# Half FFNs with seven block products on one core: token sums before the gate tile, block sums merged, product P6 one place later

## Chip, core and metric

The kernel runs on one NeuronCore of a Trainium2 chip as a hand-ordered program: TensorE (PE), VectorE (DVE), ScalarE (ACT), GpSimd (POOL) and SyncE (SP) each have their own instruction list and meet only in semaphores. The metric is the device time of one execution in microseconds.

## The reference, cut

One inference step of two layers for 512 prompt tokens and 8 sample tokens, model width 1024. The change lies in the four half FFNs alone; the mixers between them (gated linear attention with DeltaNet, stick-breaking attention with RG-LRU) stay as they are.

```python
def half_ffn(x, g, w_gate, w_up, w_down):      # width 1024 -> 2816 -> 1024
    h = rmsnorm(x, g)
    return 0.5 * ((jax.nn.silu(h @ w_gate) * (h @ w_up)) @ w_down)

for layer in range(2):
    x = x + half_ffn(x, ...)                   # both for x_prompt and x_sample
    x = x + mixer(rmsnorm(x, ...))
    x = x + half_ffn(x, ...)
y = rmsnorm(x, ln_final)
```

## The kernel before

All 520 tokens are held transposed (features on partitions) in xT. A float32 operand is split into a high part, copied by ACT (hb_h, ht_h, whi, act_h), and the rest, subtracted by DVE (hb_l, ht_l, wlo, act_l). A product of two such operands is three matmuls: high x high, high x low, low x high. A tile of 128 output features over 1024 inputs and two halves of 260 tokens is 8 x 3 x 2 = 48 matmuls. The factor rstd of the norm is applied by DVE behind the matmuls.

The stages f0 to f3 run the same list, EVENTS. **The head**: gate tile and up tile of the features n = 0 to 3, each a plain tile ("unit") with an event of its own. DVE multiplies the gate tile by rstd (`take`), ACT applies silu, DVE multiplies by the up tile (`product`), ACT copies the high part (`high`), DVE subtracts (`low`). Each pass of n also prepares one quarter of the token sums: ACT scales a row block to xb, DVE makes four sums t1 to t4 in snapT, ACT copies them to ht_h, DVE subtracts to ht_l. t_act and t_dve count these steps; a pass starts its xb only when the ht_l of the pass in front is done, since snapT and xb have one buffer.

**The groups**: from feature tile 4 on, two gate tiles (2t, 2t+1) are made by seven block products P1 to P7 for the eight of a 2 x 2 block product (9 groups in a stage, 36 in all). A product is 12 matmuls into a PSUM bank of its own, bank_of; the group is 84 matmuls. DVE adds the products up in sums counted by block_sum: U2 = P1 + P6, U3 = U2 + P7, c11 = P1 + P2, c12 = U2 + P5 + P3, c22 = U3 + P5, c21 = U3 + P4. ACT has copied P1 to snapT before (p1_copied). Then follow the two up tiles of 48 matmuls, and the next group. After tiles 11 and 21 come the down products, 16 pieces each.

The weights of a group have four batches: a (for P1, P2), b (P4), c (P6, P5), d (P3, P7). Behind the splits of a and b DVE makes two block sums of weights each (line 1600), in place in the stage buffer; c and d need them. `make` on ACT and DVE makes the next batch in line, `ahead(done, last)` makes those whose slot is free by then, `reach(done)` waits until TensorE has finished an event. Every engine works strictly by its list, so the place of `ahead` among the other calls sets the order. TensorE starts the first group of a stage when t_dve says that the token sums of all four passes are done; it starts P3 after p1_copied, P7 after U2, P4 after c11, and the next group's P1 after all seven sums.

The lines of before that matter: ACT head 1012 to 1024 (silu 1002, high 1006, xb 1020, ht_h 1023) and copy of weights 959; DVE weight split 1608, weight sums 1600, take 1665, act_l 1674, product 1684, ht_l 1692, token sums 1708 to 1715, scaling by rstd 1729, block sums 1735; TensorE units 2505, block products 2526.

Of the kernel before, what the change touches and what calls it, by code (L numbers as in the profile page):

```python
# [33 lines left out]
P = 128  # L34
# [14 lines left out]
ORDER = ("P1", "P6", "P2", "P5", "P3", "P7", "P4")  # L49
# [57 lines left out]
def build_step(nc, i, o):  # L107
# [170 lines left out]
    with ctx:  # L278
# [305 lines left out]
        U2_SUM, C11_SUM, V_SUM, C12_SUM, U3_SUM, C22_SUM, C21_SUM = range(1, 8)  # L584
        BLOCK_SUMS = 7
# [360 lines left out]
        def _(act):  # L946
# [45 lines left out]
            def ffn(s, f):  # L992
# [19 lines left out]
                def head(n, up, done):  # L1012

                    ahead(done - 1)
                    if not up:
                        silu(n)
                        act.wait_ge(x_ready, KD * (s + 1))
                        if KP * f + n:
                            act.wait_ge(t_dve, 5 * (KP * f + n))
                        act.activation(xb[:], xT[:, 2 * n, :], ACT.Copy, scale=h_scale(s, 2 * n)).then_inc(t_act, 1)  # L1020
                    else:
                        act.wait_ge(t_dve, 5 * (KP * f + n) + 4)
                        act.activation(ht_h[:, :, n, :], snapT[:], ACT.Copy).then_inc(t_act, 1)
                        high(n)

                def group_step(g, which, t, up, done, late):
# [3 lines left out]
                    if which == "P1":  # L1030
                        reach(done)
                        if q:
                            act.wait_ge(block_sum, BLOCK_SUMS * (q - 1) + C11_SUM)
                        act.activation(snapT[:, 2, :], PS[:, bank_of("P1", up), 0:HALF], ACT.Copy).then_inc(p1_copied, 1)
                        ahead(done, own - 1)
                    elif which == "P2":
                        ahead(done, own)
                        if late:
                            half_of(*late.pop())
# [4 lines left out]
                    elif which == "P7":  # L1044
                        ahead(done, own + 3)
                        half_of(2 * t, up)
                    elif which == "P4":
# [545 lines left out]
        def _(dve):  # L1593
# [74 lines left out]
            def ffn(s, f):  # L1668
# [17 lines left out]

                def head(n, up, done):

                    ahead(done - 1)
                    if up:  # L1690
                        dve.wait_ge(t_act, X_TURNED + 2 * (KP * f + n) + 2)
                        dve.tensor_tensor(ht_l[:, :, n, :], snapT[:], ht_h[:, :, n, :].bitcast(F32), ALU.subtract)\  # L1692
                           .then_inc(t_dve, 1)
                    reach(done)
                    if not up:
# [6 lines left out]
                        count, x1, g1 = 5 * (KP * f + n), xT[:, 2 * n + 1, :], h_scale(s, 2 * n + 1)  # L1702
                        t1, t2, t3, t4 = (snapT[:, m, :] for m in range(4))
                        b11, b12, b21, b22 = xb[:, 0:HALF], xb[:, HALF:TOK], x1[:, 0:HALF], x1[:, HALF:TOK]
                        dve.wait_ge(t_act, X_TURNED + 2 * (KP * f + n) + 1)
                        if count:
                            dve.wait_ge(t_dve, count)
                        dve.tensor_tensor(t1, b12, b11, ALU.subtract).then_inc(t_dve, 1)
                        dve.scalar_tensor_tensor(out=t3, in0=b22, scalar=g1, in1=b12, op0=ALU.mult, op1=ALU.subtract)\
                           .then_inc(t_dve, 1)  # L1710
                        dve.wait_ge(t_dve, count + 1)
                        dve.scalar_tensor_tensor(out=t2, in0=b22, scalar=g1, in1=t1, op0=ALU.mult, op1=ALU.subtract)\
                           .then_inc(t_dve, 1)
                        dve.wait_ge(t_dve, count + 3)
                        dve.scalar_tensor_tensor(out=t4, in0=b21, scalar=g1, in1=t2, op0=ALU.mult, op1=ALU.subtract)\
# [7 lines left out]
                def half_of(n, up, q):  # L1723

                    dve.wait_ge(block_sum, BLOCK_SUMS * q + (C21_SUM if n % 2 else C12_SUM))
# [11 lines left out]
                def group_step(g, which, t, up, done, late):  # L1737
# [3 lines left out]
                    bank = {w: PS[:, bank_of(w, up), 0:HALF] for w in PRODUCTS}  # L1741
                    u2, u3, p1 = (snapT[:, n, :] for n in range(3))
                    (c11, c12), (c21, c22) = ([tmp[:, a + 2 * up, h * HALF:(h + 1) * HALF] for h in range(2)] for a in range(2))
# [745 lines left out]
        def _(pe):  # L2489
# [40 lines left out]
            def ffn(s, f):  # L2530
# [45 lines left out]
                def group_product(g, which, t, up):  # L2576
# [10 lines left out]
                    elif which == "P7":  # L2587
                        pe.wait_ge(block_sum, BLOCK_SUMS * q + U2_SUM)
                    elif which == "P4":
                        pe.wait_ge(block_sum, BLOCK_SUMS * q + C11_SUM)  # L2590
# [737 lines left out]
```

## Time and profile before

| | us |
|---|---|
| median of 3 runs | 2202.9 |
| lowest and highest | 2197.45, 2203.23 |
| profiled execution, whole | 2199.94 |
| its span, first to last instruction | 2198.3 |
| TensorE busy | 2129.5 (97%) |
| DVE busy | 1352.5 (62%) |
| ACT busy | 861.6 (39%) |
| mean granted TensorE clock | 0.985 of full |

The profiled execution is one run of its own. Its span leaves out 1.6 us of start and end. Where TensorE is busy nearly all the time, the profile is to be read for the places where it isn't: the list of its waits, the chain of work that ended last, and then the timelines of DVE and ACT around such a place.

### The profile page before, as it was taken

To read this page: it belongs to the slowest core of one execution; us is meant where nothing else is said; L and a number is where in the kernel's file an instruction comes from. 1 tells how busy PE (TensorE), PEld (TensorE's weight loads), DVE (VectorE), ACT (ScalarE), POOL (GpSimd) and SP (SyncE) were. 2 spreads that over 40 slices of the span, in tenths; PEclk is the share of its full clock that TensorE was granted. 3 is DMA by queue.
4 is the path that set the end of the run, shared out by engine and by line. 5 is a ranking of instruction groups with operands and counts; after the bars stand their busy time and mean duration, and the time that the engine had idled before them with its cause. 6 is when DMAs were issued, how large, how long until landed. Compare 5 with 4: busy or idle time off the path is not lost.

```text
span 2198.3 us, 42097 instructions
## 1 busy us (share of the span) xinstructions
PE 2129.5 (97%) x17908; PEld 2070.3 (94%) x17908; DVE 1352.5 (62%) x2124; ACT 861.6 (39%) x1232; POOL 67.2 (3%) x140
## 2 busy tenths in 40 slices
PE   7899999999988999999999999999999999999998
PEld 7899999999978899999999999999997599999997
DVE  6763675686455557737656754675657547745754
ACT  5431332344244444313334332333457634322323
POOL 0000000100100000000000000000102300000000
PEclk9999999999998999999999999999999999999999
DMA  4332232533200333332323232332324423232321
GB/s 148 89 103 83 84 106 70 132 83 85 75 10 2 82 91 97 106 92 87 95 79 115 78 106 87 106 92 82 102 78 131 140 78 106 78 110 82 113 74 64
DMA packets 318362, 199.16 MB, mean 91 GB/s; under 512 B 10006, under 2 KB 313266, under 8 KB 318168
## 3 DMA queue, kind: packets, MB, share of 16 engines
q1 hardware_dynamic: 309840, 174.49, 27.0%
q0 software_dynamic: 6160, 19.84, 3.1%
q8 instruction: 142, 2.33, 0.4%
q10 hardware_dynamic: 2176, 2.15, 0.3%
q14 instruction: 44, 0.36, 0.1%
HBM read 188.52 MB, written 8.05 MB: 89 GB/s over the span
## 4 chain that ended last, share of the span: by engine, by line
PE 87%; DVE 7%; ACT 3%; issue 3%; DMA 0%; ACTq 0%; DVEq 0%
PE PS L2505 60%; PE PS L2526 17%; PE PS L2678 4%; DVE wlo L1608 1%; PE PS L3220 1%; ACT whi L959 1%; PE PS L3139 1%; PE PS L3153 0%; DVE ht_l L1692 0%; PE PS L3122 0%; ACT xb L1020 0%; DVE tmp L1665 0%; DVE X L2052 0%; PE PS L3205 0%; PE PS L3023 0%
## 5 line engine op out<-in xcount | busy, mean ns | idle before, releaser
L2505 PE MATMUL PS<-hb_h,whi 128*128 128x260 f32 x2448 | 498.2, 285 | 1.8 <-DVE hb_l L2430 1.8
L2505 PE MATMUL PS<-hb_h,wlo 128*128 128x260 f32 x2448 | 496.1, 284 | 0.0
L2505 PE MATMUL PS<-hb_l,whi 128*128 128x260 f32 x2448 | 493.9, 283 | 0.0
L2505 PEld LDWEIGHTS PS<-hb_h,whi 128*128 128x128 f32 x2448 | 380.7, 189 | 4.5 <-DVE wlo L1608 1.4
L2505 PEld LDWEIGHTS PS<-hb_h,wlo 128*128 128x128 f32 x2448 | 378.7, 189 | 0.0
L2505 PEld LDWEIGHTS PS<-hb_l,whi 128*128 128x128 f32 x2448 | 377.5, 189 | 0.0
L1608 DVE TENSOR_TENSOR wlo<-stage,whi 128x1024 fp32r<-128x1024 f32 (+1 forms) x193 | 232.6, 1205 | 151.1 <-ACT whi L959 145.5
L959 ACT ACTIVATE whi<-stage 128x1024 fp32r<-128x1024 f32 (+1 forms) x193 | 199.9, 1038 | 123.3 <-PE PS L2526 64.4
L1608 DVE TENSOR_TENSOR wlo<-stage_x,whi 128x1024 fp32r<-128x1024 f32 (+1 forms) x148 | 175.1, 1185 | 52.2 <-ACT whi L959 51.9
L959 ACT ACTIVATE whi<-stage_x 128x1024 fp32r<-128x1024 f32 (+1 forms) x148 | 150.8, 1022 | 133.4 <-DVE stage_x L1600 115.2
L1813 DVE SCALAR_TENSOR_TENSOR tmp<-PS,rstd 128x520 f32<-128x520 f32 x64 | 44.7, 698 | 235.8 <-PE PS L2505 235.8
L2505 PE MATMUL PS<-act_l,whi 128*128 128x260 f32 x896 | 180.8, 283 | 0.0
L2505 PE MATMUL PS<-act_h,wlo 128*128 128x260 f32 x896 | 180.1, 282 | 0.0
L2505 PE MATMUL PS<-act_h,whi 128*128 128x260 f32 x896 | 179.9, 282 | 0.0
L2526 PE MATMUL PS<-hb_h,whi 128*128 128x260 f32 x432 | 124.0, 287 | 17.5 <-DVE ht_l L1692 17.5
L2505 PEld LDWEIGHTS PS<-act_h,wlo 128*128 128x128 f32 x896 | 138.1, 188 | 0.0
L2505 PEld LDWEIGHTS PS<-act_h,whi 128*128 128x128 f32 x896 | 138.0, 188 | 0.0
L2505 PEld LDWEIGHTS PS<-act_l,whi 128*128 128x128 f32 x896 | 137.7, 188 | 0.0
L2526 PE MATMUL PS<-hb_l,whi 128*128 128x260 f32 x432 | 123.5, 286 | 0.0
L2526 PE MATMUL PS<-ht_h,whi 128*128 128x260 f32 x432 | 123.5, 286 | 0.0
L2526 PE MATMUL PS<-ht_l,whi 128*128 128x260 f32 x432 | 123.5, 286 | 0.0
L2526 PE MATMUL PS<-hb_h,wlo 128*128 128x260 f32 x432 | 123.5, 286 | 0.0
(472 smaller groups left out, 3764.2 us busy)
## 6 DMA issues: line engine op xcount, KB each, us to landing
stage<-in_ffn_w_up SPq DMA_DIRECT2D x88, 512.0 KB, 3.8
stage_x<-in_ffn_w_gate SPq DMA_DIRECT2D x36, 1024.0 KB, 5.2
stage<-in_w_in_e SPq DMA_DIRECT2D x28, 512.0 KB, 3.8
stage_x<-in_ffn_w_down SPq DMA_DIRECT2D x20, 512.0 KB, 4.2
stage<-in_ffn_w_down SPq DMA_DIRECT2D x40, 256.0 KB, 2.7
stage<-in_w_in_o SPq DMA_DIRECT2D x20, 512.0 KB, 3.8
stage<-in_ffn_w_gate SPq DMA_DIRECT2D x16, 512.0 KB, 3.8
stage_x<-in_ffn_w_down SPq DMA_DIRECT2D x20, 384.0 KB, 3.7
```

The source lines that it names most:

```text
L959: act.activation(split_out(batch, False), staged(batch), ACT.Copy).then_inc(hi_ready, 1)
L1608: dve.tensor_tensor(split_out(batch, True), staged(batch), split_out(batch, False).bitcast(F32), ALU.subtract).then_inc(lo_ready, 1)
L1813: dve.scalar_tensor_tensor(out=y, in0=psum, scalar=0.5, in1=two(rstd[:]), op0=ALU.mult, op1=ALU.mult)\
L2505: mm = pe.matmul(psum[:, half, :], w, x(k, half), start=first and w is hi and x is rhs_hi, stop=last and w is lo)
L2526: mm = pe.matmul(PS[:, bank, 0:HALF], w[:, c:c + P], x[:, j, :], start=j == 0 and n == 0, stop=j == KP - 1 and n == 2)
L2678: return pe.matmul(out, w, x, start=True, stop=True)
L3139: mm = pe.matmul(acc, upto[:], sp[:, at:at + w], start=True, stop=n == NB - 1)
L3220: return pe.transpose(dst, src, ident[0:n, 0:n])
```

## The change

Three things are changed; all that is computed stays, up to the order of additions.

1. In the head, DVE makes the token sums of pass n at the start of the event of gate tile n (new `token_sums`), before the weight batches and before `take`, and ht_l directly behind `take`. ACT makes xb first, then the weight copy that is due, then ht_h, and silu behind it.
2. The seven block sums are five. P1_SUMS adds P1 to P2 and P6 in one operation over two banks (c11 and U2 at once, U2 in the place of c12). U3, V and C12 follow behind P4, and C2_SUMS adds U3 to P4 and P5 in one (c21, c22). P7 and P4 both wait for P1_SUMS.
3. ORDER is P1, P2, P6, P5, ...: P2 and P6 change places, and their banks too. The late silu or high of the tile in front stays at the third product; silu of tile 2t comes with P4 and no longer with P7.

```diff
-ORDER = ("P1", "P6", "P2", "P5", "P3", "P7", "P4")
+ORDER = ("P1", "P2", "P6", "P5", "P3", "P7", "P4")
-            return 4 * up + {"P1": 0, "P6": 1, "P2": 2, "P5": 3, "P3": 0, "P7": 1, "P4": 2}[which]
+            return 4 * up + {"P1": 0, "P2": 1, "P6": 2, "P5": 3, "P3": 0, "P7": 1, "P4": 2}[which]
...
                 def head(n, up, done):
-                    ahead(done - 1)
                     if not up:
-                        silu(n)
                         act.wait_ge(x_ready, KD * (s + 1))
                         if KP * f + n:
                             act.wait_ge(t_dve, 5 * (KP * f + n))
                         act.activation(xb[:], xT[:, 2 * n, :], ACT.Copy, scale=h_scale(s, 2 * n)).then_inc(t_act, 1)
-                    else:
+                    ahead(done - 1)
+                    if not up:
                         act.wait_ge(t_dve, 5 * (KP * f + n) + 4)
                         act.activation(ht_h[:, :, n, :], snapT[:], ACT.Copy).then_inc(t_act, 1)
+                        silu(n)
+                    else:
                         high(n)
...
                 def head(n, up, done):
+                    if not up:
+                        token_sums(n)
                     ahead(done - 1)
-                    if up:
-                        dve.wait_ge(t_act, X_TURNED + 2 * (KP * f + n) + 2)
-                        dve.tensor_tensor(ht_l[:, :, n, :], snapT[:], ht_h[:, :, n, :].bitcast(F32), ALU.subtract)\
-                           .then_inc(t_dve, 1)
                     reach(done)
...
                         take(two(tmp[:, n % 2, :]), pair(2 * (n % 2))).then_inc(gate_read, 1)
...
+                        dve.wait_ge(t_act, X_TURNED + 2 * (KP * f + n) + 2)
+                        dve.tensor_tensor(ht_l[:, :, n, :], snapT[:], ht_h[:, :, n, :].bitcast(F32), ALU.subtract)\
                            .then_inc(t_dve, 1)
...
-                    elif which == "P2":
+                    elif which == "P6":
                         reach(done)
-                        if q:
-                            dve.wait_ge(block_sum, BLOCK_SUMS * q)
                         dve.wait_ge(p1_copied, q + 1)
-                        add(q, U2_SUM, u2, p1, bank["P6"])
                         if base + 2 * t >= 2:
                             dve.wait_ge(act_lo if up else prod_ready, base + 2 * t - 1)
-                        add(q, C11_SUM, c11, p1, bank["P2"])
+                        add(q, P1_SUMS, tile0, PS[:, first + 1:first + 3, 0:HALF], p1.to_broadcast([P, 2, HALF]))
                         ahead(done, own)
...
                     elif which == "P3":
-                        reach(done)
-                        add(q, V_SUM, c12, u2, bank["P5"], U2_SUM)
-                        add(q, C12_SUM, c12, c12, bank["P3"], V_SUM)
-                        half_of(2 * t, up, q)
                         ahead(done, own + 2)
                     elif which == "P7":
-                        reach(done)
-                        add(q, U3_SUM, u3, u2, bank["P7"])
-                        dve.wait_ge(act_lo if up else prod_ready, base + 2 * t)
-                        add(q, C22_SUM, c22, u3, bank["P5"], U3_SUM)
                         ahead(done, own + 3)
                     elif which == "P4":
                         reach(done)
-                        add(q, C21_SUM, c21, u3, bank["P4"])
+                        add(q, U3_SUM, snapT[:, 1, :], PS[:, bank_of("P7", up), 0:HALF], c12, P1_SUMS)
+                        add(q, V_SUM, c12, PS[:, bank_of("P5", up), 0:HALF], c12, U3_SUM)
+                        add(q, C12_SUM, c12, PS[:, bank_of("P3", up), 0:HALF], c12, V_SUM)
+                        dve.wait_ge(act_lo if up else prod_ready, base + 2 * t)
+                        add(q, C2_SUMS, tile1, PS[:, first + 2:first + 4, 0:HALF], u3.to_broadcast([P, 2, HALF]))
+                        half_of(2 * t, up, q)
                         half_of(2 * t + 1, up, q)
...
-                    elif which == "P7":
-                        pe.wait_ge(block_sum, BLOCK_SUMS * q + U2_SUM)
-                    elif which == "P4":
-                        pe.wait_ge(block_sum, BLOCK_SUMS * q + C11_SUM)
+                    elif which in ("P7", "P4"):
+                        pe.wait_ge(block_sum, BLOCK_SUMS * q + P1_SUMS)
```

The order on DVE in the head of f0, pass n = 1, before (take, four token sums, weight split, ht_l, product, act_l):

```order
L1665 SCALAR_TENSOR_TENSOR tmp<-PS,rstd 128x520 [waits unit_done]
L1708 TENSOR_TENSOR snapT<-xb 128x260 [waits t_dve,t_act]
L1709 SCALAR_TENSOR_TENSOR snapT<-xT,prm,xb 128x260
L1712 SCALAR_TENSOR_TENSOR snapT<-xT,prm,snapT 128x260 [waits t_dve]
L1715 SCALAR_TENSOR_TENSOR snapT<-xT,prm,snapT 128x260 [waits t_dve]
L1608 TENSOR_TENSOR wlo<-stage,whi 128x1024 [waits unit_done,hi_ready]
L1692 TENSOR_TENSOR ht_l<-snapT,ht_h 128x4x260 [waits t_act]
L1684 TENSOR_TENSOR tmp<-tmp,PS 128x520 [waits gate_ready,unit_done]
```

and after the change, from the token sums of the same pass to its product:

```order
L1696 TENSOR_TENSOR snapT<-xb 128x260 [waits t_dve,t_act]
L1697 SCALAR_TENSOR_TENSOR snapT<-xT,prm,xb 128x260
L1700 SCALAR_TENSOR_TENSOR snapT<-xT,prm,snapT 128x260 [waits t_dve]
L1703 SCALAR_TENSOR_TENSOR snapT<-xT,prm,snapT 128x260 [waits t_dve]
L1609 TENSOR_TENSOR wlo<-stage,whi 128x1024 [waits unit_done,hi_ready]
L1666 SCALAR_TENSOR_TENSOR tmp<-PS,rstd 128x520 [waits unit_done]
L1720 TENSOR_TENSOR ht_l<-snapT,ht_h 128x4x260 [waits t_act]
L1609 TENSOR_TENSOR wlo<-stage,whi 128x1024 [waits unit_done,hi_ready]
L1685 TENSOR_TENSOR tmp<-tmp,PS 128x520 [waits gate_ready,unit_done]
```

The four sums stand in front of the weight split and take, and ht_l stands behind take; the second weight split of the pass is now behind ht_l.

The order on ACT in the same pass, before (silu, xb, weight copy, ht_h, act_h, weight copy):

```order
L1002 ACTIVATE tmp<-tmp 128x520 [waits gate_read]
L1020 ACTIVATE xb<-xT,prm 128x520 [waits t_dve,x_ready]
L959 ACTIVATE whi<-stage 128x1024 [waits unit_done,w_loaded0]
L1023 ACTIVATE ht_h<-snapT 128x4x260 [waits t_dve]
L1006 ACTIVATE act_h<-tmp 128x520 [waits prod_ready]
L959 ACTIVATE whi<-stage 128x1024 [waits unit_done,w_loaded1]
```

and after:

```order
L1018 ACTIVATE xb<-xT,prm 128x520 [waits t_dve,x_ready]
L959 ACTIVATE whi<-stage 128x1024 [waits unit_done,w_loaded1]
L1022 ACTIVATE ht_h<-snapT 128x4x260 [waits t_dve]
L1002 ACTIVATE tmp<-tmp 128x520 [waits gate_read]
L959 ACTIVATE whi<-stage 128x1024 [waits unit_done,w_loaded0]
L1006 ACTIVATE act_h<-tmp 128x520 [waits prod_ready]
```

xb stands in front, silu behind ht_h. Both silu and ht_h wait for DVE.

The order on DVE in the first group, before, from U2 and c11 (rows 1 and 2) on:

```order
L1735 TENSOR_TENSOR snapT<-snapT,PS 128x260 [waits p1_copied,unit_done]
L1735 TENSOR_TENSOR tmp<-snapT,PS 128x260 [waits prod_ready]
L1608 TENSOR_TENSOR wlo<-stage,whi 128x1024 [waits unit_done,hi_ready]
L1608 TENSOR_TENSOR wlo<-stage_x,whi 128x1024 [waits unit_done,hi_ready]
L1600 TENSOR_TENSOR stage_x<-stage_x 128x4x128 [waits lo_ready]
L1600 TENSOR_TENSOR stage_x<-stage_x 128x4x128 [waits sums]
L1608 TENSOR_TENSOR w4l<-stage_x,w4h 128x512 [waits unit_done,hi_ready]
L1600 TENSOR_TENSOR stage_x<-stage_x 128x4x128 [waits sums,lo_ready]
L1600 TENSOR_TENSOR stage_x<-stage_x 128x4x128 [waits sums]
L1735 TENSOR_TENSOR tmp<-snapT,PS 128x260 [waits block_sum,unit_done]
L1735 TENSOR_TENSOR tmp<-tmp,PS 128x260 [waits block_sum]
L1729 TENSOR_TENSOR tmp<-tmp,rstd 128x520 [waits block_sum]
```

and after, from P1_SUMS (row 1) on:

```order
L1740 TENSOR_TENSOR tmp<-PS,snapT 128x520 [waits prod_ready,p1_copied,unit_done]
L1609 TENSOR_TENSOR wlo<-stage,whi 128x1024 [waits unit_done,hi_ready]
L1609 TENSOR_TENSOR wlo<-stage_x,whi 128x1024 [waits unit_done,hi_ready]
L1601 TENSOR_TENSOR stage_x<-stage_x 128x4x128 [waits lo_ready]
L1601 TENSOR_TENSOR stage_x<-stage_x 128x4x128 [waits sums]
L1609 TENSOR_TENSOR w4l<-stage_x,w4h 128x512 [waits unit_done,hi_ready]
L1601 TENSOR_TENSOR stage_x<-stage_x 128x4x128 [waits sums,lo_ready]
L1601 TENSOR_TENSOR stage_x<-stage_x 128x4x128 [waits sums]
L1609 TENSOR_TENSOR wlo<-stage_x,whi 128x1024 [waits unit_done,hi_ready]
L1740 TENSOR_TENSOR snapT<-PS,tmp 128x260 [waits block_sum,unit_done]
L1740 TENSOR_TENSOR tmp<-PS,tmp 128x260 [waits block_sum] x2
L1740 TENSOR_TENSOR tmp<-PS,snapT 128x520 [waits prod_ready]
```

One sum of 520 elements stands where U2 and c11 stood, the weight batches follow it directly, and all other block sums come behind them.

## Rows read from the trace of the kernel before

**Rows 1.** The page: busy time by engine; the chain that ended last, by engine.
```profile
PE 2129.5 (97%) x17908; PEld 2070.3 (94%) x17908; DVE 1352.5 (62%) x2124; ACT 861.6 (39%) x1232; POOL 67.2 (3%) x140
...
PE 87%; DVE 7%; ACT 3%; issue 3%; DMA 0%; ACTq 0%; DVEq 0%
```

**Rows 2.** Waits of TensorE (total us, times, longest): all, 60 to 80, 780 to 1300.
```profile
PE PS L2526 <- DVE ht_l L1692: 17.5, 4, 7.0
...
PE PS L2526 <- DVE ht_l L1692: 7.0, 1, 7.0
...
PE PS L2526 <- DVE ht_l L1692: 6.2, 2, 4.3
```

**Rows 3.** The chain in order of time: start us, us, what; behind the four heads.
```profile
75.92 11.64 PE PS L2526 x84
...
99.08 10.08 PE PS L2526 x84
...
849.39 11.87 PE PS L2526 x84
...
1221.07 11.84 PE PS L2526 x84
...
1856.84 11.87 PE PS L2526 x84
```

**Rows 4.** Windows: length, busy us of PE, PEld, DVE, ACT, POOL, PEclk, DMA share, GB/s.
```profile
1223.00:1225.00 2.00, 2.00 (x11) 2.00 (x10) 0.59 (x2) 1.33 (x2) 0.00 (x0) 0.50 0.69 246
...
880.00:1100.00 220.00, 220.00 (x1836) 220.00 (x1836) 136.17 (x194) 70.45 (x93) 0.00 (x0) 1.00 0.32 94
```

**Rows 5.** DVE in order of time in the head of f0: start us, us, what [idle before].
```profile
43.56 0.69 DVE L1684 TENSOR_TENSOR tmp<-tmp,PS 128x520 f32<-128x520 f32 x1
...
53.12 0.69 DVE L1684 TENSOR_TENSOR tmp<-tmp,PS 128x520 f32<-128x520 f32 x1
...
55.27 0.49 DVE L1638 MEMSET ssum<- 128x520 f32 x1
...
58.77 0.43 DVE L1708 TENSOR_TENSOR snapT<-xb 128x260 f32<-128x260 f32 x1 [1.32 <-ACT xb L1020]
...
60.44 1.22 DVE L1608 TENSOR_TENSOR wlo<-stage_x,whi 128x1024 fp32r<-128x1024 f32 x1
...
65.08 1.23 DVE L1692 TENSOR_TENSOR ht_l<-snapT,ht_h 128x1040 fp32r<-128x1040 f32 x1
...
74.62 1.24 DVE L1692 TENSOR_TENSOR ht_l<-snapT,ht_h 128x1040 fp32r<-128x1040 f32 x1
```

**Rows 6.** ACT in order of time in the heads of f0, f1 and f2.
```profile
36.92 1.28 ACT L990 ACT_TABLE_LOAD   x1
...
44.28 0.64 ACT L1006 ACTIVATE act_h<-tmp 128x520 fp32r<-128x520 f32 x1 [1.91 <-DVE tmp L1684]
44.83 1.04 ACT L959 ACTIVATE whi<-stage 128x1024 fp32r<-128x1024 f32 x1
...
58.02 0.71 ACT L1020 ACTIVATE xb<-xT,prm 128x520 f32<-128x520 f32 x1
...
60.56 1.08 ACT L1023 ACTIVATE ht_h<-snapT 128x1040 fp32r<-128x1040 f32 x1 [0.35 <-DVE snapT L1715]
...
807.41 1.28 ACT L990 ACT_TABLE_LOAD   x1
...
1181.42 1.28 ACT L990 ACT_TABLE_LOAD   x1
```

**Rows 7.** One group from 99.08 on, DVE and ACT; idle of DVE before line 1735 until.
```profile
103.44 0.43 DVE L1735 TENSOR_TENSOR snapT<-snapT,PS 128x260 f32<-128x260 f32 x1 [0.28 <-PE PS L2526]
...
109.65 1.42 DVE L1600 TENSOR_TENSOR stage_x<-stage_x 128x512 f32<-128x512 f32 x2
...
112.64 0.64 ACT L1002 ACTIVATE tmp<-tmp 128x520 f32<-128x520 f32 x1 [1.15 <-DVE tmp L1729]
...
  PE PS L2526: 18.8, 36
```

More of the change, by code:

```diff
@@ L583, in build_step @@
         block_sum, p1_copied = sem("block_sum"), sem("p1_copied")
-        U2_SUM, C11_SUM, V_SUM, C12_SUM, U3_SUM, C22_SUM, C21_SUM = range(1, 8)
-        BLOCK_SUMS = 7
+        P1_SUMS, U3_SUM, V_SUM, C12_SUM, C2_SUMS = range(1, 6)
+        BLOCK_SUMS = 5
         t_act, t_dve = sem("t_act"), sem("t_dve")
@@ L1037, in group_step @@
                         ahead(done, own)
-                        if late:
-                            half_of(*late.pop())
+                    elif which == "P6" and late:
+                        half_of(*late.pop())
                     elif which == "P5":
@@ L1045, in group_step @@
                         ahead(done, own + 3)
+                    elif which == "P4":
                         half_of(2 * t, up)
-                    elif which == "P4":
                         late.append((2 * t + 1, up))
@@ L1685, in product, with token_sums @@
                        .then_inc(prod_ready, 1)
+                def token_sums(n):
+                    count, x1, g1 = 5 * (KP * f + n), xT[:, 2 * n + 1, :], h_scale(s, 2 * n + 1)
+                    t1, t2, t3, t4 = (snapT[:, m, :] for m in range(4))
+                    b11, b12, b21, b22 = xb[:, 0:HALF], xb[:, HALF:TOK], x1[:, 0:HALF], x1[:, HALF:TOK]
+                    dve.wait_ge(t_act, X_TURNED + 2 * (KP * f + n) + 1)
+                    if count:
+                        dve.wait_ge(t_dve, count)
+                    dve.tensor_tensor(t1, b12, b11, ALU.subtract).then_inc(t_dve, 1)
+                    dve.scalar_tensor_tensor(out=t3, in0=b22, scalar=g1, in1=b12, op0=ALU.mult, op1=ALU.subtract)\
+                       .then_inc(t_dve, 1)
+                    dve.wait_ge(t_dve, count + 1)
+                    dve.scalar_tensor_tensor(out=t2, in0=b22, scalar=g1, in1=t1, op0=ALU.mult, op1=ALU.subtract)\
+                       .then_inc(t_dve, 1)
+                    dve.wait_ge(t_dve, count + 3)
+                    dve.scalar_tensor_tensor(out=t4, in0=b21, scalar=g1, in1=t2, op0=ALU.mult, op1=ALU.subtract)\
+                       .then_inc(t_dve, 1)
                 def head(n, up, done):
+                    if not up:
+                        token_sums(n)
                     ahead(done - 1)
-                    if up:
-                        dve.wait_ge(t_act, X_TURNED + 2 * (KP * f + n) + 2)
-                        dve.tensor_tensor(ht_l[:, :, n, :], snapT[:], ht_h[:, :, n, :].bitcast(F32), ALU.subtract)\
-                           .then_inc(t_dve, 1)
                     reach(done)
@@ L1740, in group_step @@
                     own = BY_FIRST[f, g, "a"].n + (6 if MODES[t][1] == "P" else 4)
-                    bank = {w: PS[:, bank_of(w, up), 0:HALF] for w in PRODUCTS}
-                    u2, u3, p1 = (snapT[:, n, :] for n in range(3))
-                    (c11, c12), (c21, c22) = ([tmp[:, a + 2 * up, h * HALF:(h + 1) * HALF] for h in range(2)] for a in range(2))
+                    first = 4 * up
+                    u3, p1 = snapT[:, 1:2, :], snapT[:, 2:3, :]
+                    tile0, tile1 = two(tmp[:, 2 * up, :]), two(tmp[:, 2 * up + 1, :])
+                    c12 = tmp[:, 2 * up, HALF:TOK]
                     if which == "P1":
                         ahead(done, own - 1)
-                    elif which == "P2":
+                    elif which == "P6":
                         reach(done)
-                        if q:
-                            dve.wait_ge(block_sum, BLOCK_SUMS * q)
                         dve.wait_ge(p1_copied, q + 1)
-                        add(q, U2_SUM, u2, p1, bank["P6"])
                         if base + 2 * t >= 2:
                             dve.wait_ge(act_lo if up else prod_ready, base + 2 * t - 1)
-                        add(q, C11_SUM, c11, p1, bank["P2"])
+                        add(q, P1_SUMS, tile0, PS[:, first + 1:first + 3, 0:HALF], p1.to_broadcast([P, 2, HALF]))
                         ahead(done, own)
```

19 lines of the change are left out of this document (2 added, 17 removed).

## The prediction

> **What bounds the kernel now.** The first view is busy time by engine with the chain that ended last [rows 1]. TensorE is busy for 2129.5 of 2198.3 us and carries 87% of the chain, DVE 7%. Only idle time of TensorE, or its time at a lower clock, is to be had. The list of TensorE's waits comes second [rows 2]: its largest entry is 17.5 us before the first block product (line 2526) of the four feed-forward stages, released by DVE's ht_l at line 1692. It splits into 7.0 us (stage f0), 6.2 us together in f1 and f2, and 4.3 us in f3; the last two stages of the sum are 4.3 for f1 (the longest of that answer) and 1.9 for f2. In the chain by pieces [rows 3] the 84 matmuls of a group take 10.08 us each time, but 11.64, 11.87, 11.84 and 11.87 us right behind the four stalls. The windows behind the stall of f2 show why: the granted clock is 0.50 from 1223 to 1225, that is 1.2 instead of 2.4 GHz, after 1.9 us idle, and 1.00 over 220 us of unbroken groups [rows 4]. This adds 1.56 + 1.79 + 1.76 + 1.79 = 6.9 us. The stalls thus cost 17.5 + 6.9 = 24.4 us. That is everything which the first part of the change can win.
>
> **Where the stall comes from.** TensorE may start the first group only when the token sums of all four passes are split (t_dve), so the end of the last ht_l counts. In f0 that is 75.86 [rows 5], with TensorE free since 75.92 - 7.0 = 68.9. From the product of pass 0 (starts 43.56) to the end of the last ht_l DVE takes 32.3 us for three passes. In each pass DVE idles 1.32 us for xb [rows 5], since ACT runs silu first and can do that only after DVE's take; it idles again for act_h and for a weight copy.
>
> **Part 1, token sums ahead of the gate tile.** The work stays the same; its order changes. I put the new order together from the old durations. Steps on DVE follow each other some 0.1 us before the end of the row in front, ACT's too; I use start to start. From the start of product(n): 0.69 for it, 0.64 - 0.10 for high(n), 0.71 for xb(n+1) and about 0.1 of hand-over give 2.0 us to the first token sum, and act_l now lies in that time, not ahead of it. The four sums take 60.44 - 58.77 = 1.67 us, a weight split 1.22 less the overlap, 1.15, take 0.7 (as long as the product, 520 elements from PSUM), silu 0.54 (as act_h, 0.64 less the overlap), then ACT's weight copy 1.04 [rows 5, 6] and DVE's split of it 1.15: 2.0 + 1.67 + 1.15 + 0.7 + 0.54 + 1.04 + 1.15 = 8.25 us to product(n+1), where it is 53.12 - 43.56 = 9.56 us now [rows 5]. ht_h on ACT (1.08) lies beside split and take, ht_l (1.24) beside silu and copy. From product(1) to product(2) the memset adds 0.45 (0.49 less a little) and the longer weight piece (a and b with their four block sums, 65.08 - 60.44 = 4.64 us, for 1.15) adds 3.5: 12.2 us. From product(2) to the end of ht_l(3): 2.0 + 1.67 + 1.15 + 0.6 + 1.24 = 6.7 us, because the split for d no longer stands in front. Together 8.25 + 12.2 + 6.7 = 27.15 us for 32.3.
>
> The start is the cost. xb(0) begins when the table load ends, 36.92 + 1.28 = 38.2 in f0 [rows 6], and now sums and take follow, then silu, weight copy and split: 0.75 + 1.67 + 0.7 + 0.4 (silu stands behind ht_h) + 0.6 + 1.04 + 1.15 = 6.3 us, so product(0) starts at 44.5, 0.9 us later than the 43.56 of before. The last ht_l ends at 44.5 + 27.15 = 71.65: **f0 keeps a stall of 71.65 - 68.9 = 2.75 us and saves 4.3**. In between, the third gate tile needs its weights at 68.9 - 4 x 5.76 = 45.8 (a tile has 48 matmuls of 10.08 / 84 = 0.12 us [rows 3]); the split now lands at 44.6. 1.2 us are left: cover, but thin.
>
> f1: table load over at 807.41 + 1.28 = 808.7 [rows 6], a weight piece more ahead of take, so 7.0 us to product(0) and 27.15 to the last ht_l: 842.85. TensorE is free at 849.39 - 4.3 = 845.1: 2.2 us of slack, **4.3 us saved and the clock kept, 1.79**. f3 stands to its own stall as f1 does (4.3, 11.87) and gives the same. f2: 1182.7 + 6.3 + 27.15 = 1216.15 against 1221.07 - 1.9 = 1219.2: 3 us of slack, **1.9 + 1.76 saved**. For f0 the clock is between kept and lost; the nearest row is f2, where 1.9 us idle cost 1.76, so I let f0 pay its 1.56.
>
> Sum: 4.3 + (4.3 + 1.79) + (1.9 + 1.76) + (4.3 + 1.79) = 20.1 us.
>
> The Trainium skill (TensorE: Matmul & The Clock Gate, Part 1: The HAM clock gate) advises that the ramp penalty is under 1% of a span and not to be fitted. Here it is 0.3% of the span, so the page agrees in size, yet it is over a quarter of the gain: left out, the sum would be 14.8 us.
>
> **Part 2, five sums for seven, and P6 a product later.** The path through TensorE is never held up by the block sums before: DVE idled for the end of the third product in all 36 groups, 18.8 us together, and the only wait of TensorE in line 2526 is the one for ht_l [rows 2, 7]. The merged first sum starts where U2 did, 103.44 in the group that starts at 99.08, and writes 520 elements from PSUM, as line 1684 does in 0.69 us. It ends at 104.15. P7, which waits for it, is the sixth product: 99.08 + 5 x 1.44 = 106.28. Slack 2.1 us for 2.4 before. DVE's pieces a and b still come behind it (the third order excerpt), so nothing new is in front. The other sums move behind P4: 3 x 0.42 + 0.69 and two scalings by rstd of 0.69 are 3.3 us, from about 112.8 (109.65 + 1.42 for the weight sums, the copy for c and its split) to 115.9. The banks are wanted by the next P1 at 99.08 + 10.08 + 11.52 = 120.7, two up tiles later: 4.8 us left. silu(2t) moves from 112.64 to about 115.4 and product(2t) stands behind it at about 116.1, where TensorE has finished its up tile at 109.16 + 5.76 = 114.9 [rows 3, 7]; the unit whose bank it frees is a whole group away. The last piece ahead of the next group, d, moves about 0.5 us and has over 5 us. Summed: nothing on the path; DVE loses 36 x (7 x 0.42 - 3 x 0.42 - 2 x 0.69) = 11 us of busy time, worth nothing. If the 2.1 us cover were gone, each microsecond late would cost 36. P6's weights get 1.44 us more time; they were never late, so nothing again. The queue of weight loads on SP keeps its order; slot 0 or its like comes free one product (1.44 us) sooner, which ACT uses for a copy 1.44 us earlier.
>
> The Trainium skill (Perfetto Trace Analysis, Optimizing Scalar/DVE Operations) speaks against this part: where DVE isn't saturated but makes another engine wait, splitting instructions lets work finish sooner. Merging does the reverse. By that rule the sum would be that of rival D; [rows 7] show that the condition, an engine that waits, does not hold here yet.
>
> **Rivals.**
> (B) No stall anywhere, f0 included: my 8.25 us per pass is 0.9 us too long. Against it: f0's start penalty and a chain made of measured rows. It gives 20.1 + 2.75 + 1.56 = 24.4 us, 2177.
> (C) Shorter stalls stay in f1 and f3 as well, since a hand-over or a weight copy is later than I have it by more than 2.2 us; then their clock loss stays too. Gain 4.3 + 3.7 + 2 x 2 = 12 us, 2190. For it: the slack is a sum of twenty terms. The thin 1.2 us at the third gate tile of f0 belongs here.
> (D) P7 ends up waiting for the first sum in every group, and each wait is longer by what the merged sum takes more, 0.69 - 0.42 = 0.27 us: 36 x 0.27 = 10 us given back, 2192. Against it: the 2.1 us of slack.
> (E) Slower: P7 waits for the first sum behind weight work. That needs a piece of kind a or b in front of it, 1.23 + 1.42 + 0.69 + 1.42 = 4.76 us less 2.1 of slack, 2.6 us x 36 = 95 us, 2277. It decides from 2.1 us on, and the gain is used up at 2.1 + 20/36 = 2.7 us. Against it: in the excerpt that work stands behind the sum.
> (F) The change doesn't reach the path: ACT's silu or high is really what ends the head, and product(0)'s 0.9 us recurs in each pass. Then f0 gains 1.5 us and the others 3.5 together: 2197. Against it: ACT idles between its steps of the head, since it waits for DVE's sums (0.35) [rows 6].
>
> **How the numbers follow.** The profiled run took 2199.9 us, span 2198.3; 2199.9 - 20.1 = 2179.8. The median is 3 us higher, 2202.9, which gives 2182.8. Neither is better, so 2181.5, and the rivals are counted from the same base, 2201.6. Chances: forecast 0.60, B 0.12, C 0.13, D 0.04, E 0.04, F 0.07. The range runs from B with the lowest run of before (2197.5 - 24.4 = 2173) to D and C, 2192. What a measurement of this kernel can tell from no change is about 0.3%, 6.6 us, so faster means below 2196.3: faster 0.88, same 0.07, slower 0.05.
>
> **What would show it.** In the profile after: TensorE's wait for ht_l is one entry of about 2.75 us in f0; groups behind the heads of f1, f2 and f3 take 10.08 us; DVE's idle before the first token sum is gone; three passes from product(0) to the last ht_l last some 27 us; no wait on a block sum. The forecast is wrong if line 2526 waits in 36 places, if any head unit waits for wlo, or if a group takes over 10.08 us while the head is clean.

## The result, and the profile after

| | before | after |
|---|---|---|
| median, us | 2201.65 (2197.45 to 2203.23, 4 runs) | 2178.59 (2177.07 to 2182.29, 4 runs) |
| profiled execution, whole | 2199.94 | 2179.37 |
| its span | 2198.3 | 2177.7 |
| mean granted clock | 0.985 | 0.990 |

The ratio is 0.9902, 95% interval 0.9885 to 0.9919: faster by 1%. The forecast was 2181.5, its range 2173 to 2192.

The page after, busy time by engine and the chain by engine, to be set beside [rows 1]; below it the only wait of line 2526, over the whole run, beside [rows 2]:

```profile
PE 2121.8 (97%) x17908; PEld 2062.7 (95%) x17908; DVE 1344.2 (62%) x2052; ACT 865.3 (40%) x1232; POOL 67.2 (3%) x140
...
PE 91%; DVE 5%; ACT 2%; issue 1%; DMA 0%; ACTq 0%; DVEq 0%
```

```profile
PE PS L2526 <- DVE ht_l L1720: 2.9, 1, 2.9
```

TensorE has less to wait for, so its share of the chain rises from 87 to 91%, and its busy time falls by 7.7 us although it issues the same 17908 matmuls: fewer of them run at the low clock. Four stalls of 17.5 us together have become one of 2.9 us. The chain in order of time (start, us, what) has the groups behind the four heads, beside [rows 3]; the second one is the ordinary group behind f0's:

```profile
71.66 11.86 PE PS L2526 x84
...
95.04 10.07 PE PS L2526 x84
...
837.30 10.07 PE PS L2526 x84
...
1205.25 10.08 PE PS L2526 x84
...
1838.05 10.08 PE PS L2526 x84
```

Only f0 still pays for the low clock. DVE in order of time in the head of f0 (start, us, line, operation, [idle before]), beside [rows 5]; line 1696 is the first token sum, 1685 the product, 1720 ht_l:

```profile
44.33 0.69 DVE L1685 TENSOR_TENSOR tmp<-tmp,PS 128x520 f32<-128x520 f32 x1
...
46.35 0.43 DVE L1696 TENSOR_TENSOR snapT<-xb 128x260 f32<-128x260 f32 x1
...
49.77 1.23 DVE L1720 TENSOR_TENSOR ht_l<-snapT,ht_h 128x1040 fp32r<-128x1040 f32 x1
51.51 1.23 DVE L1609 TENSOR_TENSOR wlo<-stage,whi 128x1024 fp32r<-128x1024 f32 x1 [0.51 <-ACT whi L959]
52.65 0.69 DVE L1685 TENSOR_TENSOR tmp<-tmp,PS 128x520 f32<-128x520 f32 x1
...
64.94 0.69 DVE L1685 TENSOR_TENSOR tmp<-tmp,PS 128x520 f32<-128x520 f32 x1
...
70.37 1.23 DVE L1720 TENSOR_TENSOR ht_l<-snapT,ht_h 128x1040 fp32r<-128x1040 f32 x1
```

The idle time of 1.32 us ahead of the token sums [rows 5] is gone. What is left in a pass is 0.70 us of waiting for ACT's high part of the product and 0.51 us for ACT's weight copy behind ht_l.

In one ordinary group, the merged first sum of DVE (line 1740), and behind P4 the last one, the answer on line 1740 as to what DVE waited for, beside [rows 7]:

```profile
99.39 0.70 DVE L1740 TENSOR_TENSOR tmp<-PS,snapT 128x520 f32<-128x520 f32 x1 [0.28 <-PE PS L2526]
...
109.59 0.69 DVE L1740 TENSOR_TENSOR tmp<-PS,snapT 128x520 f32<-128x520 f32 x1
...
  PE PS L2526: 16.3, 36
```

DVE still waits for the third product in all 36 groups, and TensorE never waits for the sum: its only wait in line 2526 is the one for ht_l.

### The profile page after: what moved, and what is told of

Its sections match the earlier page's. It is cut to its first block, busy times and chain, and to the rows that moved or that the text cites. A ratio compares the mean times of both kernels' runs of the same rounds, so it can differ in the third digit from the quotient of the medians.

```text
span 2177.7 us, 41989 instructions
## 1 busy us (share of the span) xinstructions
PE 2121.8 (97%) x17908; PEld 2062.7 (95%) x17908; DVE 1344.2 (62%) x2052; ACT 865.3 (40%) x1232; POOL 67.2 (3%) x140
## 4 chain that ended last, share of the span: by engine, by line
PE 91%; DVE 5%; ACT 2%; issue 1%; DMA 0%; ACTq 0%; DVEq 0%
PE PS L2505 65%; PE PS L2526 17%; PE PS L2676 4%; PE PS L3218 1%; PE PS L3137 1%; DVE wlo L1609 1%; PE PS L3151 0%; PE PS L3120 0%; DVE X L2052 0%; PE PS L3203 0%; PE PS L3140 0%; PE PS L3021 0%; ACT whi L959 0%; PE PS L2516 0%; PE PS L2744 0%
## 5 line engine op out<-in xcount | busy, mean ns | idle before, releaser
L2526 PE MATMUL PS<-ht_h,wlo 128*128 128x260 f32 x432 | 122.0, 283 | 0.0
```

Of the source, the lines that this page charges most:

```text
L2526: mm = pe.matmul(PS[:, bank, 0:HALF], w[:, c:c + P], x[:, j, :], start=j == 0 and n == 0, stop=j == KP - 1 and n == 2)
```

## Where the 20.6 us of span went

The numbers are read from the two chains in order of time. In f0 the stall ends 4.26 us sooner (71.66 against 75.92) and the first group is 0.22 us longer; f1 and f3 save 4.3 + 1.8 us each, f2 1.9 + 1.76. That is 19.9 of 20.6 us. The remaining 0.7 us is what is left of larger changes outside the heads, in code that is the same in both kernels. In the first layer the products ahead of the mixer came out 1.5 us shorter (185.44 for 186.98) and the mixer 2.2 us shorter (154.65 for 156.88). In the second layer the mixer came out 1.5 us longer (110.23 for 108.69) and so did the 432 matmuls behind it (53.43 for 51.90). In the windows over these stretches the granted clock falls at other places than before. This is looked at again below.

## The experiments

Each kernel is before or the change with the edit shown. They ran in three sets, each on one chip, with the kernel before beside them: e1 to e4 (before 2199.93, 15 runs), e5 and e6 (2197.37, 1 run), e7 to e10 (2198.68, 11 runs).

**1. Which part gives the gain.** `e1_head_only` takes from the change only the two `head` functions and `token_sums`; the block sums and ORDER are those of before. `e2_groups_only` is the rest.

> The new head alone (xb first on ACT, token sums ahead of take, ht_l behind it); order of products and the seven block sums as before. Theory: the whole gain is in the head, so 20 to 23 us below the kernel before, as the full change: one wait for ht_l of about 2.9 us in f0, none in f1, f2 and f3, and the first groups of f1 to f3 at 10.08 us. Rival (the merged sums help TensorE as well): clearly less gain than the full change, 3 us or more apart.

> The new groups alone (P6 a product later, five block sums); the head as before. Theory: nothing, within 0.2% of the kernel before; four waits for ht_l of 7.0, 4.3, 1.9 and 4.3 us and four first groups of 11.6 to 11.9 us stay, DVE is busy some 8 to 11 us less. Rival (merging gives something back or costs): 5 us or more either way, and a wait on a block sum or weights in line 2526.

| | median, us | ratio, 95% interval |
|---|---|---|
| e1_head_only | 2175.27 | 0.9891 (0.9876 to 0.9907) |
| e2_groups_only | 2200.82 | 1.0004 (0.9994 to 1.0013) |

Both expectations came true within the intervals (24.7 us for the 20 to 23 of the first), and the whole gain is the head's. TensorE's waits on ht_l, first of e1, then of e2:

```profile
PE PS L2531 <- DVE ht_l L1720: 3.0, 1, 3.0
```

```profile
PE PS L2521 <- DVE ht_l L1692: 17.5, 4, 7.1
```

**2. The place of ht_l on DVE.** In the full change ht_l goes back behind the weight work, directly ahead of the product; all else of the new order stays:

```diff
                         take(two(tmp[:, n % 2, :]), pair(2 * (n % 2))).then_inc(gate_read, 1)
-                        dve.wait_ge(t_act, X_TURNED + 2 * (KP * f + n) + 2)
-                        dve.tensor_tensor(ht_l[:, :, n, :], snapT[:], ht_h[:, :, n, :].bitcast(F32), ALU.subtract)
...
                     ahead(done - 1)
+                    if up:
+                        dve.wait_ge(t_act, X_TURNED + 2 * (KP * f + n) + 2)
+                        dve.tensor_tensor(ht_l[:, :, n, :], snapT[:], ht_h[:, :, n, :].bitcast(F32), ALU.subtract)
                     reach(done)
```

> The full change, but ht_l stands where it did, behind the second weight batch of its pass and ahead of the product. This parts the two edits in the head. Theory: the passes keep their 8.3 us, and only the last ht_l ends one split later, about 1.15 to 1.7 us (it waits for ACT's copy too): f0 waits 4.1 to 4.6 us instead of 2.9, f1 to f3 still not at all (slack was 2.3 us or more by the profile after). Rival (the place of ht_l is most of the gain): waits come back in f1 and f3, 2 us or more each with their clock loss, 8 us or more in all.

Measured 2201.86 us (one run): the expectation of +1.2 to 1.7 us failed, the rival holds, and the whole gain is gone. TensorE's waits, and one pass of DVE in f0:

```profile
PE PS L2527 <- DVE ht_l L1713: 21.4, 4, 9.3
```

```profile
48.47 0.69 DVE L1666 SCALAR_TENSOR_TENSOR tmp<-PS,rstd 128x520 f32<-128x520 f32 x1
50.82 1.23 DVE L1609 TENSOR_TENSOR wlo<-stage,whi 128x1024 fp32r<-128x1024 f32 x1 [1.65 <-ACT whi L959]
51.96 1.24 DVE L1713 TENSOR_TENSOR ht_l<-snapT,ht_h 128x1040 fp32r<-128x1040 f32 x1
53.11 0.69 DVE L1685 TENSOR_TENSOR tmp<-tmp,PS 128x520 f32<-128x520 f32 x1
```

Behind take DVE can do nothing on the product's way until ACT has done silu and the weight copy. In the change ht_l stands there, and 0.51 us of idle time are left. Here the whole 1.65 us are idle and ht_l's 1.15 us come on top. The product is thus 1.15 us later in each of the first three passes (the pass shown takes 9.46 us instead of 8.32; before it took 9.56), and the last ht_l, which TensorE waits for, also has the copy and the split in front: 8.29 us behind its product instead of 5.43. The sum, 1.15 + 1.14 + 1.17 + 2.86 = 6.3 us, matches the difference of the stalls in f0, 9.3 against 2.9. In f1 and f3 the slack of 2.1 us (experiment 4) swallows a part and 4.3 us of wait remain, to the tenth those of before; in f2 it is 3.5 us, where before had 1.9.

**3. ACT's order without DVE's.** The kernel before with the new order on ACT alone (xb, weight copy, ht_h, silu):

> Only ACT's new order in the head (xb, weight copy, ht_h, silu); DVE keeps take, token sums, weight split, ht_l of before, and the groups are those of before. It tells ACT's part of the head from DVE's. By the durations seen: product 0.69, act_l and hand-over 0.7, xb and weight copy on ACT in that time and 0.9 behind it, split 1.15, take 0.7, sums 1.67, split 1.15, ht_l 1.15: 8.7 us per pass for 9.56, and product(0) of f0 0.6 us earlier. The last ht_l comes 3.2 us sooner: waits of 3.8 us in f0, 1.1 in f1 and f3, none in f2; 11.5 us and one to three clock losses saved, 2183 to 2188. Rival: DVE's order is all of it (ht_l in the gap behind take, as its being moved away cost all that was won); then passes stay at 9.5 us and the time at 2197 to 2201.

Measured 2230.72 us, ratio 1.0141 (1.0113 to 1.0170): neither. It is 32 us **slower** than before. TensorE's waits, and a pass of DVE in f0:

```profile
PE PS L2527 <- DVE ht_l L1693: 46.2, 4, 14.5
```

```profile
52.02 0.49 DVE L1716 SCALAR_TENSOR_TENSOR snapT<-xT,prm,snapT 128x260 f32<-128x260 f32 x1
55.12 1.23 DVE L1609 TENSOR_TENSOR wlo<-stage,whi 128x1024 fp32r<-128x1024 f32 x1 [2.61 <-ACT whi L959]
56.27 1.23 DVE L1693 TENSOR_TENSOR ht_l<-snapT,ht_h 128x1040 fp32r<-128x1040 f32 x1
57.42 0.69 DVE L1685 TENSOR_TENSOR tmp<-tmp,PS 128x520 f32<-128x520 f32 x1
```

My sum of 8.7 us per pass had counted the DVE work and forgotten what stands on ACT in front of the copy that this split needs: ht_h (1.07) and silu (0.62), which begin only when DVE's last token sum is done, then the copy (1.04). DVE idles 2.61 us for it, with ht_l behind the idle time instead of in it. The pass takes 57.42 - 46.05 = 11.37 us (product to product) for 9.56. 28.7 us of the 32 are in the list of waits (46.2 against 17.5), 1.0 in the four first groups (48.2 against 47.2 us), the rest lies outside the heads.

e8 and e4 have the same order on ACT, and ht_l directly ahead of the product in both. In the heads they differ only in DVE's token sums (the groups' part is worth nothing by e2), behind take in e8 and ahead of the weight work in e4. With the sums ahead the time goes from 32 us above its kernel before to 2 us above, and f0's pass from 11.37 to 9.46 us. On the new order of ACT the early sums are thus worth some 30 us, and the place of ht_l some 22 us more; the order of ACT without the two costs 32 us. The gain belongs to the three together and can't be given to one of them. Two orders were not tried: DVE's new order with ACT's old one, and ht_l behind the product, which would tell whether it needs the wait or only has to be out of the product's way.

**4. How much room the heads have.** In the full change three more ht_l of the last pass stand ahead of the true one, each waiting for the one in front:

```diff
+                        for k in range(3 if n == 3 else 0):
+                            padded(dve.tensor_tensor(ht_l[:, :, n, :], snapT[:], ht_h[:, :, n, :].bitcast(F32), ALU.subtract))
                         dve.tensor_tensor(ht_l[:, :, n, :], snapT[:], ht_h[:, :, n, :].bitcast(F32), ALU.subtract)
```

> The full change, and DVE makes the subtraction of ht_l in pass 3 four times instead of once, in each of the four stages: 3 x 1.28 = 3.8 us later. Theory: the slack of the heads is 2.3 us (f1, f3) and 3 us (f2), so waits of about 6.7 us in f0, 1.5 us in f1 and f3 and 0.9 us in f2, and each of them costs the clock behind it too (first groups of 11.6 to 11.9 us instead of 10.08). Sum: 3.8 + 1.5 + 0.9 + 1.5 + 3 x 1.8 = 13 us above the full change. Rival (a stall under 2 us leaves the clock up): the same waits, first groups of f1 to f3 at 10.08 us, 8 us above.

Measured 2190.99 us (one run), 12 us over the change, for the 13 expected. The waits came out near the expectation (1.8 for 1.5 us, 1.0 for 0.9), the clock did not: the expectation had it fall behind all of them, the rival behind none in f1 to f3. The waits are 6.8 us in f0 (+3.9, the full delay), and in f1, f2 and f3:

```profile
PE PS L2536 <- DVE ht_l L1730: 1.8, 1, 1.8
...
PE PS L2536 <- DVE ht_l L1730: 1.0, 1, 1.0
```

(f3 has 1.8 again.) With 3.9 us of delay the slack is 3.9 - 1.8 = 2.1 us in f1 and f3 and 2.9 in f2; the prediction had 2.2 and 3. The first groups are 12.24, 11.84, 10.34 and 10.34 us. Waits (11.4 against 2.9) and groups (44.76 against 42.09) make 8.5 + 2.7 = 11.2 of the 11.6 us. The windows show f1, then f3 (length, busy us of PE, PEld, DVE, ACT, POOL, PEclk, DMA share, GB/s):

```profile
842.00:844.00 2.00, 0.66 (x6) 0.46 (x4) 1.97 (x2) 0.00 (x0) 0.00 (x0) 1.00 0.00 0
844.00:846.00 2.00, 1.53 (x8) 1.54 (x9) 2.00 (x3) 0.00 (x0) 0.00 (x0) 0.67 0.05 12
846.00:848.00 2.00, 2.00 (x11) 2.00 (x11) 0.85 (x2) 1.33 (x3) 0.00 (x0) 0.50 0.52 127
1846.00:1848.00 2.00, 0.70 (x6) 0.49 (x5) 1.97 (x2) 0.00 (x0) 0.00 (x0) 1.00 0.00 0
1848.00:1850.00 2.00, 1.50 (x12) 1.50 (x13) 2.00 (x3) 0.00 (x0) 0.00 (x0) 1.00 0.00 0
1850.00:1852.00 2.00, 2.00 (x19) 2.00 (x18) 0.88 (x2) 1.78 (x4) 0.00 (x0) 1.00 0.46 103
```

Both stages idle 1.8 us. Behind it the clock is at its lower level (1.2 GHz) in f1 and stays at 2.4 GHz in f3. Idle time of this size may or may not cost the clock; in f2, where 1.0 us were idle, it stayed up too.

**5. How much room the first block sum has, and what a repeated wait costs.** In front of P1_SUMS stand 4, 6 or 8 dependent additions of 260 elements each in a part of snapT that is free then, in all 36 groups:

```diff
+                        for k in range(4):
+                            padded(dve.tensor_tensor(snapT[:, 0, :], snapT[:, 2, :], snapT[:, 2, :], ALU.add))
                         add(q, P1_SUMS, tile0, PS[:, first + 1:first + 3, 0:HALF], p1.to_broadcast([P, 2, HALF]))
```

> The full change, and in each of the 36 groups four extra DVE sums of 260 elements stand in front of the first block sum: 4 x 0.45 = 1.8 us later. Theory: P7 has 2.1 us of slack for that sum, so no wait in line 2526 but the one of f0, and the time of the full change within 3 us. Rival (the sum is on the path already): 36 x 1.8 = 65 us more.

> As the run with four, with six extra sums in front of the first block sum: 2.7 us later, 0.6 us past the slack. Theory: 36 waits of about 0.6 us before P7, 20 us above the full change with the clock up. Rival (each such wait pulls the clock down as in the heads): 36 x (0.6 + 1.8) = 86 us above.

> As above with eight extra sums: 3.6 us later, 1.5 us past the slack. Theory: 36 waits of about 1.5 us, 54 us above the full change with the clock up. Rival (the clock falls with each, as behind the 1.9 us wait of f2 in the kernel before): 36 x (1.5 + 1.8) = 119 us above.

| additions | us (one run each) | over the change's profiled run |
|---|---|---|
| 4 | 2179.43 | 0.1 |
| 6 | 2213.30 | 33.9 |
| 8 | 2247.20 | 67.8 |

TensorE's waits for the sum, with 6 and then with 8 additions; 4 have none:

```profile
PE PS L2536 <- DVE tmp L1748: 24.7, 36, 0.7
```

```profile
PE PS L2536 <- DVE tmp L1748: 58.1, 36, 1.6
```

Two additions make 0.93 us per group (58.1 - 24.7 over 36), one 0.46. Six are 2.78 us and the wait is 0.69 (24.7 / 36), so the slack of P7 is 2.1 us, as forecast. The idle time also came out near 20 and 54 us. But these were the forecasts of the whole loss, and that was 33.9 and 67.8 us, 14 us more than forecast each time. The runs are 33.9 - 24.7 = 9.2 and 67.8 - 58.1 = 9.7 us longer than their idle time: each wait costs about **0.26 us more than its idle time**, in both runs. The chain shows where, with 6 additions and with 8 alike: the 24 matmuls behind the wait take 3.15 us, where 24 of an ordinary group take 2.88 (10.08 x 24/84).

```profile
103.82 3.15 PE PS L2536 x24
```

It is also what a first group with the clock kept has over 10.08 us (10.34 in experiment 4, 10.33 below). And 36 waits of 1.6 us, one in each group, cost no clock; the window over seven of the groups with 8 additions:

```profile
880.00:1100.00 220.00, 208.72 (x1727) 207.24 (x1726) 148.64 (x221) 66.45 (x86) 0.00 (x0) 1.00 0.31 94
```

**6. The last stall.** f0's first xb needs no rstd, only x. In the change, and later in the head part alone, it is made ahead of the norm, and `head` leaves it out where s and n are both 0:

```diff
             make()
+            act.wait_ge(x_ready, KD)
+            act.activation(xb[:], xT[:, 0, :], ACT.Copy, scale=h_scale(0, 0)).then_inc(t_act, 1)
             for s, (name, f) in enumerate(STAGES):
                 norm(s)
```

> The full change, and in f0 ACT makes xb of pass 0 before the norm instead of behind its last table load. Theory: the 2.9 us stall that f0 keeps comes from the late start of pass 0. The sums of pass 0 are then done before rstd, ht_h starts at the end of the table load (38.1), silu 1.0 later, weight copy and split behind it: product(0) at 41.7 instead of 44.3, the last ht_l 2.6 us sooner, stall 0.3 us or none; 2.6 us less than the full change, and 4.4 us less if the clock stays up as well. Rival (the head is bound elsewhere, by weights or by take waiting for TensorE): the last ht_l moves by under 1 us and the time stays that of the full change.

> The head part alone, and the xb of f0's first pass made before the norm instead of behind the table load; the groups are those of before. Theory: parts add up. The head alone keeps one stall in f0 (3.0 us in its trace) and a first group of 11.86 instead of 10.08 us; with the early xb the same head had a wait of 0.4 us and a first group of 10.33 us in the trace of the other run. So 2.6 + 1.5 = 4.1 us below the head alone of this call. Rival: what f0 gains is given back in the stretches up to the first mixer, and the two stay within 1.5 us, as the medians of the call before had it (2176.33 with both changes and early xb, 2175.27 for the head alone).

> The full change again, on the same chip as the head alone. Theory: the groups' part is worth nothing also on top of the head, and the difference between 2178.6 (full change) and 2175.3 (head alone) lies between chips and in the mixers: the two within 1 us of each other here. Rival: with the stalls gone the merged sums cost something, and the full change is 2 to 4 us above the head alone again.

> The head part alone again, the groups of before. Theory: the same as the full change within 1 us, 0.990 of before. Rival: 2 to 4 us below the full change.

| | median, us | lowest, highest | ratio, 95% interval |
|---|---|---|---|
| e3: change + early xb (first set) | 2176.33 | 2174.57, 2177.62 | 0.9898 (0.9883 to 0.9913) |
| e9: change | 2179.30 | 2179.09, 2179.86 | 0.9908 (0.9889 to 0.9926) |
| e10: head alone | 2177.63 | 2175.22, 2181.03 | 0.9900 (0.9880 to 0.9921) |
| e7: head alone + early xb | 2172.75 | 2171.63, 2172.93 | 0.9876 (0.9854 to 0.9898) |

e7 is the best kernel of the study, 26 us below the kernel before and 6.5 below the change on the same chip. Its wait, and f0's first group:

```profile
PE PS L2534 <- DVE ht_l L1723: 0.4, 1, 0.4
```

```profile
69.08 10.33 PE PS L2534 x84
```

The stall goes from 2.9 to 0.4 us and the group from 11.86 to 10.33, clock kept: 2.5 + 1.53 = 4.0 us. By the medians of e7 and e10 it is 4.9; the runs of the two don't overlap, the intervals of their ratios do. e3 shows the same two rows (0.4 and 10.33), and its median is 2.3 us below the change's of another set, for 2.6 to 4.4 expected. Yet it is 1.1 us above that of e1, the head alone in the same set. The traces place this at the very start, ahead of f0's stall: e1's matmuls behind the loading of x start at 22.5 us and e3's at 24.7, since the first pairs of matmuls, from 13 to 18 us, take 0.64 us each in e3 and 0.40 in e1 (the column of the granted clock has 1.00 in both, so the reason stays open). e10 is the same kernel as e1 and behaves like e3 there (24.7). Differences of 1 to 2 us between the medians of two kernels are within this noise.

**Does the groups' part cost something on top of the head?** On the same chip the change (e9) is 1.7 us above the head alone (e10), though within the spread of e10's runs. The expectation had them within 1 us of each other, the rival 2 to 4 us apart; it is neither. The traces place it. The first units behind the second mixer, change then e10, in the chain:

```profile
1743.42 53.43 PE PS L2505 x432
```

```profile
1743.49 51.89 PE PS L2510 x432
```

Both start within 0.1 us, and the 432 matmuls take 1.5 us more in the change, at a mean clock of 0.91 instead of 1.00 from 1740 to 1760. e6_first_sum_late4 has all block sums of the change, and more work, and shows 51.89 us too. Over all traces both lengths occur with either kind of groups: 53.4 us in the change, e9, e4, e5, e8 and e6 with 8 additions, 51.9 in before, e1, e2, e3, e7, e10 and e6 with 4 and 6. So the 1.5 us go with where the clock falls, and not with the sums. What sets that place stays open; whether a faster or slower way through the groups shifts it was not tried.

## Why the prediction was right, point by point

| step | forecast | measured |
|---|---|---|
| product(0) of f0, behind the end of the table load | 6.3 us, at 44.5 | 44.33 - 38.04 = 6.3 |
| pass 0 to 1 | 8.25 | 52.65 - 44.33 = 8.32 |
| pass 1 to 2 | 12.2 | 64.94 - 52.65 = 12.29 |
| product(2) to the end of the last ht_l | 6.7 | 71.60 - 64.94 = 6.66 |
| stall of f0 | 2.75 | 2.9 |
| stalls of f1, f2, f3 | none | none |
| slack there | 2.2, 3, 2.2 | 2.1, 2.9, 2.1 (experiment 4) |
| first groups of f1, f2, f3 | 10.08 | 10.07, 10.08, 10.08 |
| clock loss of f0 | kept | kept, group 11.86 |
| slack of P7 | 2.1 | 2.1 (experiment 5) |
| part 2 | nothing | 1.0004 (0.9994 to 1.0013) |
| gain, profiled run | 20.1 | 20.6 |

The chain was put together from durations of single operations in the old trace, each with its overlap, and with the new order of both engines. Its steps hold beyond f0: in f1 product(0) starts 7.07 us behind the end of the table load (807.94 - 800.87), for a forecast of 7.0. Experiments 2 and 3 show what carries it: early sums and an ht_l that lies in DVE's wait for silu and copy, both on the new order of ACT. The prediction has the second in half a sentence ("ht_l (1.24) beside silu and copy"), and the price when that is not so was never worked out; my expectation of e4 then put it at less than a tenth of its size. A reader who went only by the 1.32 us of idle time for xb would have believed that early sums alone earn the gain. They do not: e4 has them, with ACT's new order, and ends 2 us above before.

That the total is met to 0.5 us is in part luck. The heads gave 19.9 us for 20.1, and that is the chain's merit; the other 0.7 us are what changes of 3.8 and 3.1 us in opposite directions outside the heads left over, and no term of the prediction covers these.

**Terms that were off.** The prediction took a first group of 11.64 to 11.87 us for clock loss throughout. 0.26 us of it belong to any wait inside the groups' matmuls (experiment 5), so the clock accounts for 1.3 to 1.5 us; the sum is not changed, since both go together when the wait goes. DVE's busy time falls by 8.3 us for the 11 forecast, worth nothing either way. The chance of the third gate tile's weights being late (1.2 us of cover) did not come true: TensorE's only wait for wlo in its units is one of 1.4 us between 13 and 20 us, in f0's first tile while x is still being loaded, and before has it too.

The median of before against that of after gives 23.1 us for a forecast of 20.1 from the traces; the interval, 0.9885 to 0.9919 or 18 to 25 us, holds both.

**Rivals.** B (no stall in f0) was wrong by the 2.9 us, and nearly came true with the early xb (e3, e7, a wait of 0.4 us). C needed a delay of over 2.2 us in f1 and f3: with 3.9 us (experiment 4) the waits came, at 2191 for its 2190, though f3 kept its clock. D and E needed P7 to be late: its price was 36 times what is beyond 2.1 us, plus 9 us for the 36 waits, which neither rival had; experiment 5 forced this delay, and the change itself has no such wait. F (silu or the high part really ends the head, the change does not reach the path) is what e4 and e8 look like, 2202 and 2231: ACT's copy behind silu does end the head's pass there. It was rejected for the right row, ACT's idle time between its steps, but with a wrong idea of what keeps it from happening.

The Trainium skill (Perfetto Trace Analysis, Optimizing Scalar/DVE Operations) advises breaking up instructions where DVE is not saturated and makes another engine wait. The merged sums do the reverse and cost nothing (e2), because the second half of that condition does not hold: TensorE begins to wait only 2.1 us later (experiment 5).

## What to carry to other kernels

When an engine runs strictly by its list, look for the place where it must wait for another engine anyway, and put there the work that nobody waits for yet; one step further on the same operation cost its whole length here, and the wait stayed empty beside it (1.65 us idle and 1.15 us more). Reordering two engines that hand work back and forth is one change: write both lists side by side and, for every wait, add up what stands in front of the awaited step on the other engine, since a part of such a change can lose more than the whole wins (32 us against 21 here). Where the work in front of a deadline doesn't need the slow input (xb here, which needs no rstd), start it before that input.

## What the runs showed of the hardware that I had not expected

- A wait of TensorE in the middle of a stream of matmuls costs its idle time and about 0.26 us more: 9.2 and 9.7 us over 36 waits of 0.69 and of 1.61 us (24 matmuls in 3.15 for 2.88 us), and 10.33 or 10.34 us for 10.08 in a group behind a wait with the clock kept. Why the matmuls behind it take longer was not tested.
- Whether idle time costs the clock is not told by its length alone: 1.9 us behind the old f2 and 1.8 us in f1 of experiment 4 did, 1.8 us in f3 of the same run did not, nor did 36 waits of 1.6 us. The Trainium skill (TensorE: Matmul & The Clock Gate, Part 1: The HAM clock gate) calls the point at which the clock rises behind a kernel's start run-variable, since the hardware's watch is not tied to that start. The pair f1 and f3 would fit the same cause for its fall, but no run here tests it.
- Outside the code that was changed, the length of a mixer and of the products beside it moved by 1.5 to 2.2 us a stretch, with granted clock at 0.91 in one trace and 1.00 in the other over the 432 matmuls shown. The spread of the times is not a mark of the kernel either: the change repeated its trace to 0.1 us in another set (the first group of f3 at 1838.05 and 1838.02), and its runs lie within 0.8 us in one set and 5.2 us apart in the other; those of the head alone lie within 0.6 us (e1) and 5.8 us apart (e10).
